# Norm roots of three head norms: spread to all rows by one rounded pass instead of a full-precision one, and the stick-breaking steps placed one tile later

## The chip, the cores and the metric

One core of one Trainium2 chip. The metric is the device time of one launch in microseconds (us), lower is better.

## The reference, cut to what matters

One decoder layer on 256 tokens of width 2048, all float32. `h = RMSNorm(x)`, one wide projection `h @ w_in` (32 column tiles of 128 for the mixers, then 48 for the gates), three mixers, a gated merge, `w_out`, and a gated MLP. What the change touches is the RMS norm over each head's 128 features, in two places: on the HGRN2 output, and on the stick-breaking mixer's queries and keys (QK-norm).

```python
# HGRN2 output, heads of 128
o = o * lax.rsqrt(jnp.mean(o * o, axis=-1, keepdims=True) + EPS)
# stick-breaking attention
qh = rms_norm(heads(q), q_g)
kh = rms_norm(heads(k), k_g)
z = jnp.einsum('bhqd,bhnkd->bhqnk', qb, kb) * scale
log_keep = jnp.where(mask, jax.nn.log_sigmoid(-z), 0.0)
within = lax.cumsum(log_keep, axis=4, reverse=True) - log_keep
w = jnp.where(mask, jnp.exp(jax.nn.log_sigmoid(z) + within + later[..., None]), 0.0)
```

## The kernel before, in words

**Layout and stream.** Features lie on the 128 partitions, tokens along the free axis. All weights stream from HBM in pieces of 128x1024 float32 through a ring of four buffers. For each piece ScalarE (ACT) writes a rounded copy `w_hi` in fp32r (line 711), VectorE (DVE) writes the rest `w_lo = raw - w_hi` (line 1024), and TensorE (PE) multiplies both parts. A wide-projection tile is two pieces; from tile 8 on it is 48 matmuls of 256 columns (line 368). In this text `lo(p)` is the w_lo operation of piece p; tile n reads pieces 2n and 2n+1.

**The order of the work.** Everything of the three mixers is put by hand between the 80 tiles of the wide projection. The table `AT` (line 92) gives each mixer product the tile after which PE issues it: `mixers(n)` of PE runs right after the matmuls of tile n. On ACT and DVE a loop over n does first the two pieces 2n+4 and 2n+5 (so they work two tiles ahead), then the eviction of tile n, then their own `mixers(n+1)`. So a result that DVE makes in `mixers(n+1)` can stand in front of lo(2n+6), which PE needs at the start of tile n+3. Every engine runs its queue in order; nothing overtakes.

**Small operations.** In DVE and ACT code each operation that a later one on the same engine depends on is issued with `link`: a semaphore increment and a wait for it before the next instruction.

**The level products.** `lev0` to `lev8` of HGRN2 stand after tiles 12, 14, 16 ... 28. For level k DVE multiplies two factors (lines 1227 and 1228), which PE waits for (line 413 is the helper that issues all full-precision products). Between tiles 7 and 16 DVE also computes the token norm, scales the first groups and x (lines 1040, 1217), splits the scaled x into `a_in` (line 1257), and does the S5 constants (`s_t`, lines 1048, 1051, 1055).

**The head norms.** `ss` (after tile 31) sums the squares of HGRN2's output, q and k: each head's sums stand on all 32 rows of its row group 32h..32h+31, with 3x256 columns (`NORM_V`). ACT takes ln and exp(-0.5 ln) in its steps 33 and 34, and DVE makes one Newton step in step 35 (`inverse_root`, three operations of 128x768, line 1048 and twice line 1055), giving `NORM_Y`. `qk_rb` after tile 35 and `hg_rb` after tile 39 (line 489) spread one row of each group over all 128 partitions with a matmul of 32 rows: weights `first_rows` (1 in the first row of each 32, else 0, set by five POOL memsets), moving data `NORM_Y` in float32. `qk_rb` has 8 such products (q and k, four heads) and `hg_rb` 4; a float32 matmul appears as two records in the trace. The four heads use four different row groups and four different PSUM banks. DVE then scales q and k (line 1273) or HGRN2's output (line 1286).

**The stick-breaking steps.** `z0`, `z1` after tile 37; ACT copies them out in step 38 (line 813) and takes abs, exp and ln(1+.) of 128x1536 with two table loads; DVE in step 39 makes softplus and log-sigmoid (line 1055, 128x1536, twice) and masks four slices (line 1048, in place on tmp); in step 40 come, in the order of the code, the scaling of HGRN2's output (line 1286, twice) and `softp_lo` (twice); `hg_out` (line 1055, four times) in step 41. `within0`, `within1` stand after tile 41, the subtraction (line 1314) in step 42, the exp in ACT's step 42, the mask `sb_w` in DVE's step 43, and `sb_o` after tile 44. The S5 states use DVE in steps 44 to 49 (rotation, scans, rotation back) behind `bu0`, `bu1`, which stand after tile 43; `o_split` is in DVE's step 48. Products alternate between two PSUM pairs in the order of `AT`, and a product waits until the one two places before it was read.

**Buffers.** `T[i]` are seven 128x1024 scratch slots of `tmp`. `NORM_Y` is in T[6]. T[4] holds the masks' index data in the first steps, HGRN2's factors later, and the softplus from DVE's step 39 on.

Of the kernel before, what the change touches and what calls it, by code (L numbers as in the profile page):

```python
# [38 lines left out]
F32 = mybir.dt.float32  # L39
F32R = mybir.dt.float32r  # L40
I32 = mybir.dt.int32
U8 = mybir.dt.uint8
ALU = mybir.AluOpType
ACT = mybir.ActivationFunctionType

P = 128
HALF = P // 2
D_MODEL = 2048
SEQ = 256
BW = D_MODEL // 4  # L50
HEADS = BW // P
# [37 lines left out]
assert all(x % RING == 0 for x in (GLU_P, BR_P, OUT_P, UP_P, DOWN_P, GLU_T, BR_T, OUT_T, UP_T, DOWN_T))  # L89


AT = {"norm1": 7, "s5_bT": 20, "hg_vT": 15, "hg_o": 30, "ss": 31, "sb_vT": 34, "qk_rb0": 35, "qk_rb1": 35, "hg_rb0": 39, "hg_rb1": 39,
      "z0": 37, "z1": 37, "within0": 41, "within1": 41, "sb_o": 44}
AT.update({f"lev{k}": 12 + 2 * k for k in range(LEVELS + 1)})
STATES_AT = (43, 46, 51, 54, 59, 62, 67, 70)
AT.update({f"bu{k}": STATES_AT[k - k % 2] for k in range(8)})
# [36 lines left out]
def layer(nc, xT, w_in, w_glu, w_br, w_out, w_up, w_down, norm_mix, norm_ffn, hg_gain, s5_small, s5_b, s5_c,  # L133
          s5_skip, sb_gain, conv, out):
    ctx = ExitStack()
    with ctx:
        def sb(name, shape, dt=F32, scope=None):
            return (scope or ctx).enter_context(nc.sbuf_tensor(name, shape, dt))
# [4 lines left out]
        w_lo = [sb(f"w_lo{s}", [P, PIECE * P], F32R) for s in range(RING)]  # L143
        half = [sb(f"half{s}", [P, SEQ]) for s in range(2)]
        ones = sb("ones", [P, P], F32R)
        first_rows = sb("first_rows", [P, P])
        eye = sb("eye", [P, P])
        upper = sb("upper", [P, P])
        lower = sb("lower", [P, P], F32R)
# [34 lines left out]
        s5_bT = sb("s5_bT", [P, 2, CT, P], F32, early)  # L184
# [7 lines left out]
        within = ExitStack()  # L192
        sb("below_within", [P, 3 * CT * SEQ + 2 * 1024], F32, within)
        softp_hi = sb("softp_hi", [P, 2 * 1024], F32R, within)
        softp_lo = sb("softp_lo", [P, 2 * 1024], F32R, within)
        within.close()
        splits = ExitStack()
        gated = sb("gated", [P, 6, SEQ], F32, splits)
# [18 lines left out]
        s5_b_in, s5_bb = proj1[:, 1, :, :], flat(proj1[:, 2, :, :])  # L217
        T = [tmp[:, i, :] for i in range(7)]
        T4 = [t.rearrange("p (c t) -> p c t", c=4) for t in T]
        NORM_V, NORM_Y, NORM_T1 = T[2][:, 0:3 * SEQ], T[6][:, 0:3 * SEQ], T[0][:, 0:3 * SEQ]  # L220
        T2 = [tmp[:, i, :].rearrange("p (s t) -> p s t", t=P) for i in range(7)]


# [9 lines left out]
        def S(name):  # L233
            if name not in sems:
                sems[name] = ctx.enter_context(nc.semaphore(name))
            return sems[name]
# [10 lines left out]
        def link(eng, ins, name):  # L247

            counts[name] = counts.get(name, 0) + 1
            ins.then_inc(S(name), 1)  # L250
            eng.wait_ge(S(name), counts[name])
# [94 lines left out]
        def _(pe):  # L346
# [99 lines left out]
            def mixers(n):  # L446
# [32 lines left out]
                for name, parts in (("qk_rb", (1, 2)), ("hg_rb", (0,))):  # L479
                    if n == AT[name + "0"]:  # L480

                        pe.wait_ge(S("norms_rstd"), 1)
                        pe.wait_ge(S("first_rows"), 1 + HEADS)
                        outs_ = [start_product(f"{name}{e}") for e in range(2)]
                        for c, part in enumerate(parts):
                            for h in range(HEADS):
                                rows = slice(32 * h, 32 * h + 32)
                                at = 512 * (h % 2) + c * SEQ
                                mm = pe.matmul(outs_[h // 2][:, at:at + SEQ], first_rows[rows, :], NORM_Y[rows, part * SEQ:(part + 1) * SEQ],
                                               start=True, stop=True, skip_group_check=True)  # L490
                                if part == parts[-1] and h % 2:
                                    mm.then_inc(product_done, 1)
# [23 lines left out]
                if n == AT["sb_o"]:  # L516
# [5 lines left out]
                    for h in range(HEADS):  # L522
                        at = 768 * (h // 2)
# [4 lines left out]
                for c in range(CT):  # L528
                    if n == AT[f"bu{2 * c}"]:
# [4 lines left out]
                        outs_ = [start_product(f"bu{2 * c + e}") for e in range(2)]  # L534
                        for r in range(2):
                            for i in range(4):
                                rows = slice(32 * i, 32 * i + 32)
# [145 lines left out]
        def bc(x, shape):  # L683
            return x.broadcast_to(shape)
# [12 lines left out]
        def s5v(name):  # L697
            return s5_t[:, SIDX[name], :]
# [5 lines left out]
        def _(act_e):  # L704
# [15 lines left out]
            def run(name, out_, in_, func, **kw):  # L720
                link(act_e, act_e.activation(out_, in_, func, **kw), name)  # L721
# [19 lines left out]
            def mixers(n):  # L741
# [62 lines left out]
                    run("norms_root", NORM_Y, NORM_V, ACT.Ln)  # L804
                if n == AT["ss"] + 3:
                    run("norms_root", NORM_Y, NORM_Y, ACT.Exp, scale=-0.5)
                if n == AT["sb_vT"] + 1:
                    wait_product(act_e, "sb_vT")
                    taken(act_e.activation(flat(HG_QQ), product("sb_vT")[:, :], ACT.Copy), "sb_vT")
# [208 lines left out]
        def _(ve):  # L1018
# [38 lines left out]
            def inverse_root(name, v, y, t):  # L1057

                ve.wait_ge(S(name + "_root"), 2)
                tt(name + "_newton", t, y, y, ALU.mult)  # L1060
                stt(name + "_newton", t, t, -0.5, v, ALU.mult, ALU.mult)
                stt(name + "_rstd", y, t, 1.5, y, ALU.add, ALU.mult)
# [29 lines left out]
            def exp_scale(out_):  # L1092

                c, n_, p = "s5_setup", s5v("t1"), s5v("t3")
                bits = s5v("r").bitcast(I32)
                ts(c, n_, n_, -126.0, 127.0, ALU.max, ALU.min)
                ts(c, bits, n_, 127.0, None, ALU.add)
                ts(c, bits, bits, 23, None, ALU.logical_shift_left)
                stt(c, out_, p, 1.0, s5v("r"), ALU.add, ALU.mult)
# [74 lines left out]
            def mixers(n):  # L1174
# [22 lines left out]
                if n == 7:  # L1197
                    masks(2)
                    exp_scale(s5v("mag"))
                if n == 12:  # L1200
                    ve.wait_ge(S("late_landed"), 16 * 9)
                    s5_angle()
# [61 lines left out]
                    ts("sb_gain", gain_sb[:, 0:1], gain_sb[:, 0:1], P ** -0.5, None, ALU.mult)  # L1264
                if n == AT["ss"] + 4:
                    inverse_root("norms", NORM_V, NORM_Y, NORM_T1)
                if n == AT["qk_rb0"] + 1:
                    for e in range(2):
                        wait_product(ve, f"qk_rb{e}")
                        heads = slice(2 * e, 2 * e + 2)  # L1270
                        rb = product(f"qk_rb{e}").rearrange("p (h c t) -> p c h t", h=2, c=2)
                        for c, x in enumerate((SQ, SK)):
                            ins = ve.scalar_tensor_tensor(x[:, heads, :], x[:, heads, :], gain_sb[:, c:c + 1], rb[:, c], ALU.mult, ALU.mult)
                            if c == 0:
                                issue(ins, "q_normed")
                            else:
                                taken(ins, f"qk_rb{e}")
                    settle(ve, "q_normed")
                    for e in range(2):
                        wait_taken(ve, f"qk_rb{e}")  # L1280
# [299 lines left out]
        def _(pool):  # L1580
            def tt(name, out_, a, b, op):
                link(pool, pool.tensor_tensor(out_, a, b, op), name)
# [1 line left out]

            link(pool, pool.memset(ones[:, :].bitcast(F32), 1.0), "ones")
            link(pool, pool.memset(s5_cT[:, :, :, :, :], 0.0), "s5_zero")
            link(pool, pool.memset(first_rows[:, :], 0.0), "first_rows")
            for h in range(HEADS):
                link(pool, pool.memset(first_rows[32 * h:32 * h + 1, :], 1.0), "first_rows")
            link(pool, pool.memset(T[3], 0.0), "hg_ex0")  # L1590
            ints = T[4].bitcast(I32)
            for c, (step, mult) in enumerate(((1, -1), (1, 0), (0, 1), (0, 1))):
# [136 lines left out]
```

## Time and profile before

| what | value |
|---|---|
| median of 3 runs | 1402.86 us (1402.77 to 1404.02) |
| the profiled execution | 1402.92 us, its span on the core 1401.4 us |
| granted TensorE clock | 1.000 of full speed over the span |
| busy shares PE, DVE, ACT, POOL | 99%, 74%, 54%, 10% |
| matmul records | 9682 |
| DMA mean | 187 GB/s |

The profile gives, for one execution, each instruction's start and duration, what each engine waited for, and the chain of work that ended last. Starts of matmuls are recorded, their ends are modelled: two matmuls in a row overlap in the table, so the distance between starts is what a matmul costs.

### The profile page before, as it was taken

The page shows a single profiled execution, that of the slowest core. Times are in us where ns is not written, and L with a number is a line of the kernel's source. Part 1 is how long each engine was busy: PE and PEld are TensorE (multiplying, and loading weights), DVE is VectorE, ACT ScalarE, POOL GpSimd, SP SyncE. Part 2 cuts the span into 40 slices and gives each one's busy share as a digit, 9 for nine tenths or more (in the row PEclk, how much of TensorE's full clock was granted, in tenths as well). Part 3 has the DMA queues.
Part 4 walks back from the last instruction along what each step waited for, and adds up shares of the span by engine and source line. Part 5 has one row for each costly group of instructions (what it writes and reads, how often), then busy time and mean ns, then how long its engine had stood idle before and what let it go on. Part 6 is the DMA issues. An engine that isn't in the chain of part 4 may idle for free.

```text
span 1401.4 us, 27481 instructions
## 1 busy us (share of the span) xinstructions
PE 1394.3 (99%) x9682; PEld 1285.5 (92%) x9682; DVE 1030.6 (74%) x1409; ACT 754.0 (54%) x1050; POOL 143.4 (10%) x190
## 2 busy tenths in 40 slices
PE   9999999999999999999999999999999999999999
PEld 8999999999999999988888888888888888888888
DVE  7898866699898777776687777777777776445453
ACT  7584777654543454545555555555555554344332
POOL 1200000000000014322111111111111110000000
PEclk9999999999999999999999999999999999999999
DMA  8654545454555556665556656656656656666663
GB/s 280 191 181 168 162 153 184 147 168 165 189 178 174 195 171 223 223 192 194 170 197 196 189 186 192 192 180 193 191 187 193 190 177 194 208 185 202 194 206 109
DMA packets 75935, 261.66 MB, mean 187 GB/s; under 512 B 8736, under 2 KB 9280, under 8 KB 75872
## 3 DMA queue, kind: packets, MB, share of 16 engines
q1 hardware_dynamic: 74304, 256.41, 57.0%
q0 software_dynamic: 1424, 4.37, 1.1%
q8 instruction: 44, 0.72, 0.2%
q14 instruction: 19, 0.16, 0.0%
q10 hardware_dynamic: 144, 0.01, 0.0%
HBM read 258.66 MB, written 2.10 MB: 186 GB/s over the span
## 4 chain that ended last, share of the span: by engine, by line
PE 91%; DVE 6%; ACT 2%; DMA 1%; issue 0%; SPq 0%; ACTq 0%; DVEq 0%
PE bank L354 40%; PE bank L368 22%; PE bank L356 21%; PE bank L394 5%; DVE w_lo L1024 2%; PE pair L413 1%; PE bank L379 1%; DVE a_in L1257 0%; ACT gates L721 0%; ACT w_hi L711 0%; DMA x_first<-xT 0%; DVE tmp L1055 0%; DVE tmp L1048 0%; DVE x_first L1217 0%; ACT tmp L721 0%
## 5 line engine op out<-in xcount | busy, mean ns | idle before, releaser
L1024 DVE TENSOR_TENSOR w_lo<-raw,w_hi 128x1024 fp32r<-128x1024 f32 x496 | 584.6, 1189 | 305.3 <-ACT w_hi L711 301.5
L711 ACT ACTIVATE w_hi<-raw 128x1024 fp32r<-128x1024 f32 x496 | 508.3, 1030 | 417.0 <-PE bank L356 198.9
L354 PE MATMUL bank<-h,w_hi 128*128 128x512 f32 x1408 | 488.4, 390 | 0.0
L356 PE MATMUL bank<-h,w_lo 128*128 128x256 f32 x1408 | 397.1, 282 | 0.0
L368 PE MATMUL bank<-a_in,w_hi 128*128 128x256 f32 x2048 | 363.1, 281 | 0.5 <-DVE w_lo L1024 0.5
L368 PEld LDWEIGHTS bank<-a_in,w_hi 128*128 128x128 f32 x2048 | 311.8, 188 | 5.3 <-issue 4.6
L354 PEld LDWEIGHTS bank<-h,w_hi 128*128 128x128 f32 x1408 | 264.2, 188 | 55.4
L368 PE MATMUL bank<-a_in,w_lo 128*128 128x256 f32 x1024 | 285.5, 279 | 0.0
L356 PEld LDWEIGHTS bank<-h,w_lo 128*128 128x128 f32 x1408 | 266.1, 189 | 0.0
L354 PE MATMUL bank<-act,w_hi 128*128 128x512 f32 x660 | 228.8, 390 | 0.0
L368 PEld LDWEIGHTS bank<-a_in,w_lo 128*128 128x128 f32 x1024 | 192.5, 188 | 0.0
L356 PE MATMUL bank<-act,w_lo 128*128 128x256 f32 x660 | 186.1, 282 | 0.0
L354 PEld LDWEIGHTS bank<-act,w_hi 128*128 128x128 f32 x660 | 123.8, 188 | 26.0
L356 PEld LDWEIGHTS bank<-act,w_lo 128*128 128x128 f32 x660 | 124.7, 189 | 0.0
L1653 POOL TENSOR_TENSOR padded<-sum_u,rstd 128x256 f32<-128x256 f32 x88 | 73.7, 838 | 413.3 <-DVE sum_u L1045 400.5
L354 PE MATMUL bank<-a_in,w_hi 128*128 128x512 f32 x256 | 88.8, 390 | 0.0
L356 PE MATMUL bank<-a_in,w_lo 128*128 128x256 f32 x256 | 72.2, 282 | 0.0
L964 ACT ACTIVATE silu<-convd 128x256 f32<-128x256 f32 x43 | 17.9, 417 | 96.0 <-DVE convd L1512 96.0
L1510 DVE SCALAR_TENSOR_TENSOR convd<-padded,taps,convd 128x256 f32<-128x256 f32 x88 | 62.6, 712 | 1.0 <-ACT convd L984 1.0
L1512 DVE SCALAR_TENSOR_TENSOR convd<-padded,taps,convd 128x256 f32<-128x256 f32 x88 | 53.9, 613 | 11.5
L354 PEld LDWEIGHTS bank<-a_in,w_hi 128*128 128x128 f32 x256 | 48.0, 188 | 10.0
L718 ACT ACTIVATE half<-bank 128x256 f32<-128x256 f32 x135 | 49.2, 365 | 3.8 <-PE bank L356 3.7
(222 smaller groups left out, 1370.3 us busy)
## 6 DMA issues: line engine op xcount, KB each, us to landing
raw<-w_up SPq DMA_DIRECT2D x176, 512.0 KB, 3.8
raw<-w_in SPq DMA_DIRECT2D x156, 512.0 KB, 4.3
raw<-w_down SPq DMA_DIRECT2D x80, 512.0 KB, 4.2
raw<-w_out SPq DMA_DIRECT2D x32, 512.0 KB, 4.2
raw<-w_br SPq DMA_DIRECT2D x16, 512.0 KB, 3.5
raw<-w_br SPq DMA_DIRECT2D x16, 256.0 KB, 3.4
raw<-w_down SPq DMA_DIRECT2D x16, 256.0 KB, 2.7
x_first<-xT SPq DMA_DIRECT2D x8, 256.0 KB, 6.6
```

Source lines behind the costliest of these rows:

```text
L354: pe.matmul(bank[b][:, :], w[:, k * P:(k + 1) * P], a.rearrange("p a t -> p (a t)"), start=first and n == 0, stop=False, skip_group_check= ...
L356: mm = pe.matmul(bank[b][:, 0:SEQ], l[:, k * P:(k + 1) * P], a[:, 0, :], start=False, stop=last and n == len(blocks) - 1, skip_group_check ...
L368: mm = pe.matmul(bank[n % BANKS][:, 0:SEQ], x[:, k * P:(k + 1) * P], src[:, PIECE * h + k, part, :], start=h == 0 and k == 0 and m == 0, s ...
L379: mm = pe.matmul(bank[b][:, 0:SEQ], x[:, k * P:(k + 1) * P], rhs(k, part), start=first and k == 0 and m == 0, stop=last and k == blocks - ...
L394: mm = pe.matmul(bank[b][:, 0:SEQ], x[:, cols], src[:, k, part, :], start=k == 0 and m == 0, stop=k == CT - 1 and m == 2, skip_group_check ...
L711: act_e.activation(w_hi[s][:, 0:blocks * P], raw[s][:, 0:blocks * P], ACT.Copy).then_inc(hi_ready, 1)
L718: act_e.activation(half[j % 2][:, :], bank[j % BANKS][:, SEQ:2 * SEQ], ACT.Copy).then_inc(half_copied, 1)
L964: act_e.activation(silu[:, :], convd[:, (j - 3) % 4, :], ACT.Silu).then_inc(S("silu_done"), 1)
L1024: ve.tensor_tensor(w_lo[s][:, w], raw[s][:, w], w_hi[s][:, w].bitcast(F32), ALU.subtract).then_inc(lo_ready, 1)
L1510: ve.scalar_tensor_tensor(c, padded[:, j % 2, 1:SEQ + 1], taps[:, t, 1:2], c, ALU.mult, ALU.add).then_inc(S("tap1"), 1)
L1512: ve.scalar_tensor_tensor(c, padded[:, j % 2, 0:SEQ], taps[:, t, 0:1], c, ALU.mult, ALU.add).then_inc(S("conv_done"), 1)
L1653: pool.tensor_tensor(padded[:, j, 2:], sum_u[:, j, :], rstd[:, :], ALU.mult).then_inc(S("up_scaled"), 1)
```

## The change

It does four things. (1) The weights become `two_rows`, in fp32r: 1 in the first row of each group of 32, -1 in the second, 0 elsewhere. DVE makes them in its step 9, from the row index that POOL left in T[4], with seven linked operations: six on 128x1 and one on 128x128. The five POOL memsets of `first_rows` go. (2) The root is kept as a rounded part and a remainder: ACT copies `NORM_Y` rounded into `NORM_HI` (128x768) in step 36, and DVE writes `norm_rows = NORM_Y * second_row + NORM_HI` (128x768) in its step 36, which holds hi in the first row and -(lo) in the second. One fp32r matmul of 32 rows then gives hi + lo. (3) `qk_rb` and `hg_rb` read `norm_rows`, so each of the 12 products is one fp32r pass. (4) `qk_rb` goes from tile 35 to 36, `z0`/`z1` from 37 to 38, `within0`/`within1` from 41 to 42 and `sb_o` from 44 to 45, with all ACT and DVE steps that are given relative to them. `hg_rb` stays at 39. `NORM_Y` moves to T[4], `norm_rows` is in T[6], `NORM_HI` in T[5].

```diff
-AT = {"norm1": 7, "s5_bT": 20, "hg_vT": 15, "hg_o": 30, "ss": 31, "sb_vT": 34, "qk_rb0": 35, "qk_rb1": 35, "hg_rb0": 39, "hg_rb1": 39,
-      "z0": 37, "z1": 37, "within0": 41, "within1": 41, "sb_o": 44}
+AT = {"norm1": 7, "s5_bT": 20, "hg_vT": 15, "hg_o": 30, "ss": 31, "sb_vT": 34, "qk_rb0": 36, "qk_rb1": 36, "hg_rb0": 39, "hg_rb1": 39,
+      "z0": 38, "z1": 38, "within0": 42, "within1": 42, "sb_o": 45}
...
-        first_rows = sb("first_rows", [P, P])
+        two_rows = sb("two_rows", [P, P], F32R)
+        second_row = sb("second_row", [P, 1])
...
+        norm_rows = sb("norm_rows", [P, 1024], F32R, within)
...
-        NORM_V, NORM_Y, NORM_T1 = T[2][:, 0:3 * SEQ], T[6][:, 0:3 * SEQ], T[0][:, 0:3 * SEQ]
+        NORM_V, NORM_Y, NORM_T1 = T[2][:, 0:3 * SEQ], T[4][:, 0:3 * SEQ], T[0][:, 0:3 * SEQ]
+        NORM_HI, NORM_ROWS = softp_lo[:, 1024:1024 + 3 * SEQ], norm_rows[:, 0:3 * SEQ]
...
-                        pe.wait_ge(S("norms_rstd"), 1)
-                        pe.wait_ge(S("first_rows"), 1 + HEADS)
+                        pe.wait_ge(S("norm_rows"), 1)
+                        pe.wait_ge(S("two_rows"), 7)
...
-                                mm = pe.matmul(outs_[h // 2][:, at:at + SEQ], first_rows[rows, :], NORM_Y[rows, part * SEQ:(part + 1) * SEQ],
+                                mm = pe.matmul(outs_[h // 2][:, at:at + SEQ], two_rows[rows, :], NORM_ROWS[rows, part * SEQ:(part + 1) * SEQ],
                                                start=True, stop=True, skip_group_check=True)
...
+                if n == AT["ss"] + 5:
+                    act_e.wait_ge(S("norms_rstd"), 1)
+                    run("norm_hi", NORM_HI, NORM_Y, ACT.Copy)
...
+                if n == 9:
+                    row, part, first = (T[4][:, (c + 1) * P - 1:(c + 1) * P] for c in (2, 3, 4))
+                    row, part = row.bitcast(I32), part.bitcast(I32)
+                    for size in (HALF, P // 4):
+                        ts("two_rows", part, row, float(size), float(size), ALU.is_ge, ALU.mult)
+                        tt("two_rows", row, row, part, ALU.subtract)
+                    ts("two_rows", second_row[:, :], row, 1.0, -1.0, ALU.is_equal, ALU.mult)
+                    ts("two_rows", first, row, 0.0, None, ALU.is_equal)
+                    tt("two_rows", two_rows[:, :], bc(first, [P, P]), bc(second_row[:, 0:1], [P, P]), ALU.add)
...
+                if n == AT["ss"] + 5:
+                    ve.wait_ge(S("norm_hi"), 1)
+                    stt("norm_rows", NORM_ROWS, NORM_Y, second_row[:, 0:1], NORM_HI.bitcast(F32), ALU.mult, ALU.add)
...
-            link(pool, pool.memset(first_rows[:, :], 0.0), "first_rows")
-            for h in range(HEADS):
-                link(pool, pool.memset(first_rows[32 * h:32 * h + 1, :], 1.0), "first_rows")
```

## Rows read from the trace of the kernel before

**Rows 1.** The page, part 1: busy time of each engine.
```profile
PE 1394.3 (99%) x9682; PEld 1285.5 (92%) x9682; DVE 1030.6 (74%) x1409; ACT 754.0 (54%) x1050; POOL 143.4 (10%) x190
```
**Rows 2.** Waits of PE: who was waited for, us in total, times, longest.
```profile
PE pair L413 <- DVE tmp L1228: 1.6, 3, 1.2
...
PE bank L368 <- DVE w_lo L1024: 0.5, 1, 0.5
```
**Rows 3.** Chain that ended last, 53 to 109 us: start, us, what.
```profile
53.80 5.67 PE bank L368 x48
...
65.16 1.13 DVE proj L1040
...
108.45 0.61 DVE tmp L1228
```
**Rows 4.** Timeline of DVE and PE, 93 to 110 us.
```profile
93.60 0.69 DVE L1228 TENSOR_TENSOR tmp<-tmp 128x512 f32<-128x512 f32 x1
...
94.48 1.15 PE L413 MATMUL pair<-tmp 128*64 128x64 f32 x32
...
109.11 1.15 PE L413 MATMUL pair<-tmp 128*64 128x64 f32 x32 [1.19 <-DVE tmp L1228]
```
**Rows 5.** Timeline of DVE, small linked operations.
```profile
27.51 0.17 DVE L1051 TENSOR_SCALAR s_t<-s_t 128x16 f32<-128x16 f32 x1
27.72 0.17 DVE L1055 SCALAR_TENSOR_TENSOR s_t<-s_t,s_in 128x16 f32<-128x16 f32 x1
...
46.31 0.28 DVE L1051 TENSOR_SCALAR tmp<-tmp 128x64 int32<-128x64 int32 x1
46.63 0.48 DVE L1048 TENSOR_TENSOR tmp<-tmp 128x64 int32<-128x64 int32 x2
...
215.51 0.15 DVE L1051 TENSOR_SCALAR gain_sb<-gain_sb 128x1 f32<-128x1 f32 x1
215.70 2.36 DVE L1024 TENSOR_TENSOR w_lo<-raw,w_hi 128x1024 fp32r<-128x1024 f32 x2
```
**Rows 6.** Timeline of PE around the two spreading products.
```profile
230.84 0.27 PE L368 MATMUL bank<-a_in,w_lo 128*128 128x256 f32 x1
231.04 1.15 PE L489 MATMUL pair<-tmp,first_rows 32*128 32x256 f32 x16
232.12 0.50 PE L368 MATMUL bank<-a_in,w_hi 128*128 128x256 f32 x2
...
257.44 0.71 PE L489 MATMUL pair<-tmp,first_rows 32*128 32x256 f32 x8
258.09 0.51 PE L368 MATMUL bank<-a_in,w_hi 128*128 128x256 f32 x2
```
**Rows 7.** Timeline of DVE and ACT, 228 to 236 us.
```profile
228.72 1.95 DVE L1055 SCALAR_TENSOR_TENSOR tmp<-tmp 128x768 f32<-128x768 f32 x2
...
232.17 0.36 ACT L739 ACTIVATE gates<-bank 128x256 f32<-128x256 f32 x1
...
235.31 1.06 ACT L711 ACTIVATE w_hi<-raw 128x1024 fp32r<-128x1024 f32 x1 [2.77 <-PE bank L368]
```
**Rows 8.** Chain that ended last, 243 to 273 us: start, us, what.
```profile
243.69 2.63 PE pair L413 x16
...
255.47 2.36 DVE w_lo L1024 x2
...
264.53 5.85 PE bank L368 x48
270.37 2.29 PE pair L413 x16
```
**Rows 9.** Timeline of DVE behind the masks, 265 to 273 us.
```profile
265.44 1.27 DVE L1286 TENSOR_TENSOR proj<-proj,pair 128x512 f32<-128x512 f32 x2
266.80 1.95 DVE L1048 TENSOR_TENSOR softp_lo<-tmp,softp_hi 128x768 fp32r<-128x768 f32 x2
...
271.06 2.04 DVE L1055 SCALAR_TENSOR_TENSOR proj<-proj,gain_hg 128x256 f32<-128x256 f32 x4
```

## The prediction, made before the changed kernel ran

> **What bounds the kernel now.** The page's first part says it at once: PE is busy 99% of the span, DVE 74% and ACT 54% [rows 1]. So I read next what PE waits for. All its waits on DVE together are a few us, of which two kinds bear on this change: 1.6 us in three waits for the level factors of line 1228, the longest 1.2, and one wait of 0.5 us for a `w_lo` [rows 2]. The average share hides what these two are, so I read the chain that ended last. For most of the span it is PE's own matmuls, one wide tile being 48 matmuls in 5.67 us, 0.118 us each [rows 3]. In two stretches it leaves PE. From 59.95 us the chain runs down DVE alone, operation behind operation; in the view it is DVE from 65.16 to the end of line 1228 at 109.06, and PE's level product starts at 109.11 after waiting 1.19 us [rows 3, 4]. The level product before it stands in the same way right behind DVE: line 1228's operation begins at 93.60 and, if it takes 0.61 us as its like in the chain does, ends by 94.3, PE begins at 94.48 [rows 3, 4]. The second stretch begins with the end of `z1` at 246.32, goes over ACT's chain and DVE's softplus and masks, and comes back to PE at 264.53, where tile 41 starts 0.5 us late [rows 2, 8]. So the question for each edit is whether it lies on PE, on one of these two DVE stretches, or beside them.
>
> **Setting up two_rows: 1.55 us, on the path.** Seven linked operations enter DVE's step 9, which is the stretch that begins before line 1040 at 65.16 [rows 3]. Six are on one column. The nearest row is one column too: it starts at 215.51 and the next operation at 215.70, so 0.19 us a step. With 16 columns a step is 0.21 (27.51 to 27.72) [rows 5]. The two `is_ge, mult` on integers are dearer: at 64 columns the step is 0.32 (46.31 to 46.63), against 0.24 to 0.26 for the integer subtraction beside it, so I add 0.05 for each [rows 5]. That is 6 x 0.19 + 2 x 0.05 = 1.24. The seventh has 128 columns and two inputs: on the line between the 0.24 of 64 columns [rows 5] and the 0.61 of 512 [rows 3] lies 0.3, which I take. Sum 1.55; bounds 1.4 and 1.7. DVE has no idle time from there to 109 that could take it, so `lev2`'s factors come 1.55 later, and `lev1`'s too. PE then waits 1.55 us more at `lev1`, and is late by just that when it comes to `lev2`; the two delays are one and the same and are not added. On the way the `w_lo` of tile 11 gets late by a few tenths as well, inside the same 1.55. The five memsets that POOL loses free nothing: POOL is at 10% [rows 1], and what DVE reads of its index data in its first steps is there long before.
> The Trainium skill (VectorE: DVE Perf Modes, the section on the TRN2 errata) gives a float32 tensor_tensor (N+151)/0.96 ns. As an estimate by that page this sum would be 6 x 0.16 + 0.29 = 1.25 us. The rows of one column stand above it, so I stay with them.
>
> **The spreading products: 0.58 us less for qk_rb, 0.3 for hg_rb.** With 16 records of `qk_rb` between them, two wide matmuls start 1.28 us apart (230.84 to 232.12); less the usual 0.12 it costs 1.16. For 8 records of `hg_rb` the next wide matmul starts 0.65 behind the first [rows 6]. The difference, 232.12-231.04 against 258.09-257.44, is 0.43 for 8 records, so 0.054 a record, and about 0.2 remain for entering and leaving, whatever the number. A float32 record of 256 columns with all rows costs about 0.22 (`z`, 8 of 256 and 8 of 128 columns in 2.63 us [rows 8]), so 0.054 is four row groups at work side by side. An fp32r one with all rows costs 0.118, four side by side 0.03. I take that: `qk_rb` 16 x 0.054 - 8 x 0.03 = 0.62, rounded down to 0.58 for its first loads, `hg_rb` half, 0.3. The bounds: no fp32r product of 32 rows is in the trace; if their groups do not overlap, `qk_rb` costs 8 x 0.118 = 0.94 instead of 0.86 and the gain is a loss of 0.1; if each can't start faster than 0.054 behind the other, the gain is 0.43 and 0.22.
> The Trainium skill (TensorEngine Tiling (Array Packing), Key Properties) says that a change of tiling mode drains the engine. By it the 0.2 us stay at both places with half or a quarter of the work between; the trace agrees, as its part that does not depend on the count shows.
>
> **The root's split: nothing.** ACT's copy of 128x768 comes behind the eviction at 232.17, and ACT then idles 2.77 us up to 235.31 for PE: under 1 us fits in. DVE's `norm_rows` is one 128x768 of 0.98 us [rows 7], and waits for the copy. It ends at about 234.5 in the time of before, and PE, without `qk_rb` behind tile 35, ends tile 36 at about 231.1 + 5.7 = 236.8: 2.3 us to spare. Behind the waiting DVE instruction stands lo(76), whose `w_hi` is not made before 235. If that cover were gone, the copy and the combination would cost up to 1.8. The scaling of q and k then follows a tile later, with a whole tile more before `z0`.
>
> **The tile later: 1.45 us on the path from z to the next w_lo.** `z0`/`z1` stand behind tile 38 instead of 37, and all of ACT's chain moves with them unchanged. What does not move is `hg_rb`, at 39. Before, DVE did softplus and masks in step 39, then lo(82), lo(83), then in step 40 the scaling of line 1286. Now softplus and masks are in step 40 too, and the code of line 1286 stands in front of them. DVE arrives there at 257.83 (255.47 + 2.36) in the time of before [rows 8]; ACT's logarithm stands ahead of the `w_hi` that this `w_lo` waited for, so it is done and nothing covers line 1286. It costs 266.80 - 265.44 = 1.36 [rows 9], and about 0.1 of waiting for `hg_rb`, which PE starts at 257.44 [rows 6] and now needs 0.4 us for. The path from `z1` to the `w_lo` behind the masks, now lo(84), thus grows by 1.45. Between them PE has as before three tiles and `hg_rb`, but 0.3 less of it. So PE's wait, now before tile 42, is 0.5 + 1.45 + 0.3 = 2.25 us in place of 0.5, and the 0.3 us of `hg_rb` are given back in it.
> What is late next: after lo(84), DVE does lo(85), `hg_out` and `softp_lo`, 1.1 + 2.1 + 2.0 us [rows 9], and is ready 5.1 us after tile 42 starts, 0.7 before PE wants `within` at 5.8. Then lo(86), lo(87) end at 7.4, `within` takes 2.29 [rows 8], tile 43 starts at 8.1: covered. The subtraction ends at about 11.6, `bu0` wants it at 13.8. The mask of `sb_w` (1.8) now stands in front of `bu0`'s rotation, and by my count the following `w_lo` have 2 us or more to spare each. `o_split` goes a step later into a lighter one. All DMA loads wait for a `w_lo` four pieces before theirs and move with them; nothing else is on SP's queue, and POOL issues none here.
>
> **Sum.** 1.55 + 1.45 - 0.58 = +2.4 us. The profiled execution was 1402.92 with a span of 1401.4, 0.06 above the median of 1402.86; so 1405.3 on either footing. A measurement of this kernel can tell about 0.2%, 2.8 us, from no change, so this is a small loss just inside "same".
>
> **Rivals.**
> A. *The row groups do not overlap in fp32r.* For it: no such product in the trace. Against: the float32 ones overlap, and so it is hardly a matter of type. `qk_rb` then gives +0.1 in place of -0.58, and with half a tenth more for the entry the sum is +3.1: 1406.0, slower by 0.22%. It decides from about 0.085 us a pass on. Chance 0.08.
> B. *softp_lo comes too late for within.* Place: DVE between lo(84) and `softp_lo`, where only 0.7 us are to spare. If ACT's w_hi(85) or the rounding of the softplus comes 1.7 us later than counted, PE waits 1 us more: +3.4, 1406.3, slower. Against: both are issued before they are needed in the trace of before. Chance 0.15.
> C. *The stretch of step 9 has slack after all* and takes the set-up: -1.55, so +0.85, 1403.7. Against: the chain is DVE without a break, and two PE waits stand right behind it. Chance 0.1.
> D. *Line 1286 hides*, since DVE gets to it while ACT's chain still runs: then -1.45, so +0.95, 1403.8. It would need ACT to be late by over 1 us. Chance 0.1.
> E. *Both hide*: -0.9 us, 1402.0. Still no faster by 0.2%. Chance 0.03.
> The forecast itself has 0.54. Its terms' own bounds are 0.15 for the set-up, 0.15 for `qk_rb`, 0.2 for line 1286, and the runs of before spread by 1.2 us; a fifth of it lies above 2.8. Slower by over 0.2%: 0.08 + 0.15 + a fifth of 0.54, in all 0.33 or so. Faster by over 0.2% needs 2.8 us that no row offers: 0.02. The rest, 0.65, is the same. The range takes in C and D below and B above, with a few tenths for the measurement: 1403.4 to 1406.8.
>
> **What would show it.** The profile after should show: seven small DVE operations of 1.5 to 1.6 us in all between 65 and 67 us, and `lev2` at about 110.7 with its wait as before or `lev1` with a longer one; 12 records of line 489's product instead of 24, the 8 of `qk_rb` in 0.5 us; line 1286 directly before the two 128x1536 operations; and one PE wait for `w_lo` of about 2.2 us where 0.5 was. PE's waits on DVE in all then rise from 2.1 (1.6 and 0.5) to about 5.4. I am wrong if the level products do not move, if the wait before tile 42 is under 1 us, or if a new wait stands before `within`.

## The result, and the profile after

| kernel | median us | ratio to the kernel before, 95% interval |
|---|---|---|
| before | 1402.86 (5 runs beside the changed one) | |
| changed | 1413.60 (1412.89 to 1414.72, 5 runs) | 1.0075 (1.0064 to 1.0087) |

The change costs 10.7 us (0.75%, clear of the noise) where 2.4 were forecast, and lies outside the range (1403.4 to 1406.8). The profiled execution has a span of 1411.5 us against 1401.4. The page of the changed kernel begins so (part 1, busy time; compare [rows 1]):

```profile
PE 1402.2 (99%) x9670; PEld 1283.3 (91%) x9670; DVE 1033.1 (73%) x1417; ACT 754.7 (53%) x1051; POOL 142.3 (10%) x185
```

PE has 12 records less, as announced, and is busy 7.9 us *longer*. That is the first sign of the miss: waits would not show as busy time. PE's waits are next (who was waited for, us in total, times, longest; compare [rows 2]):

```profile
PE bank L371 <- DVE w_lo L1030: 2.5, 2, 2.1
PE pair L416 <- DVE tmp L1243: 2.2, 3, 1.2
...
PE bank L357 <- DVE w_lo L1421: 0.6, 2, 0.4
```

On DVE they rise from 2.1 (1.6 and 0.5, the two kinds of the forecast) to 4.7 us, where 5.4 were forecast. The mechanisms of the forecast are there, and can be checked one by one. The seven set-up operations on DVE (timeline of the changed kernel; columns start, duration, engine, line, operation, tiles):

```profile
64.24 0.14 DVE L1057 TENSOR_SCALAR tmp<-tmp 128x1 int32<-128x1 int32 x1
64.42 0.16 DVE L1054 TENSOR_TENSOR tmp<-tmp 128x1 int32<-128x1 int32 x1
...
65.37 0.29 DVE L1054 TENSOR_TENSOR two_rows<-tmp,second_row 128x128 fp32r<-128x128 f32 x1
65.70 1.22 DVE L1046 TENSOR_TENSOR proj<-proj,rstd 128x1024 f32<-128x1024 f32 x1
```

From 64.24 to 65.70 they take 1.46 us; the forecast said 1.55. PE feels the delay in two places before `lev2` (timeline of PE in the changed kernel):

```profile
52.56 0.59 PE L416 MATMUL pair<-proj,ones 128*128 128x256 f32 x2
...
70.48 0.47 PE L371 MATMUL bank<-a_raw,w_hi 128*128 128x256 f32 x2 [0.37 <-DVE w_lo L1030]
...
94.97 1.15 PE L416 MATMUL pair<-tmp 128*64 128x64 f32 x32 [0.37 <-DVE tmp L1243]
...
109.74 1.15 PE L416 MATMUL pair<-tmp 128*64 128x64 f32 x32 [1.24 <-DVE tmp L1243]
```

The forecast had a few tenths at the `w_lo` of tile 11 (here 70.48) and 1.55 more at `lev1` (94.97); it is 0.37 at each. Counted from the start of `norm1`'s product (52.56 here, 53.20 before), `lev1` comes 1.1 us later than before and `lev2` 1.3. The spreading products on PE (timeline; compare [rows 6]):

```profile
237.69 0.28 PE L371 MATMUL bank<-a_in,w_lo 128*128 128x256 f32 x1
237.89 0.51 PE L492 MATMUL pair<-norm_rows,two_rows 32*128 32x256 f32 x8
238.33 0.50 PE L371 MATMUL bank<-a_in,w_hi 128*128 128x256 f32 x2
...
258.11 0.39 PE L492 MATMUL pair<-norm_rows,two_rows 32*128 32x256 f32 x4
258.43 0.51 PE L371 MATMUL bank<-a_in,w_hi 128*128 128x256 f32 x2
```

Between two wide matmuls `qk_rb` now takes 0.64 us in place of 1.28, `hg_rb` 0.32 in place of 0.65 from its first record on: 0.64 and 0.33 saved. The single records of the first four products, one for each row group, start at 0, 3, 6 and 10 ns: they overlap. Line 1286 of before, now 1304, in front of softplus, and PE's wait (timeline of DVE, then of PE; compare [rows 8, 9]):

```profile
263.95 1.28 DVE L1304 TENSOR_TENSOR proj<-proj,pair 128x512 f32<-128x512 f32 x2
265.33 3.55 DVE L1061 SCALAR_TENSOR_TENSOR tmp<-tmp 128x1536 f32<-128x1536 f32 x2
...
270.75 2.36 DVE L1030 TENSOR_TENSOR w_lo<-raw,w_hi 128x1024 fp32r<-128x1024 f32 x2
273.03 2.04 DVE L1061 SCALAR_TENSOR_TENSOR proj<-proj,gain_hg 128x256 f32<-128x256 f32 x4
275.10 1.95 DVE L1054 TENSOR_TENSOR softp_lo<-tmp,softp_hi 128x768 fp32r<-128x768 f32 x2
```
```profile
272.12 0.48 PE L371 MATMUL bank<-a_in,w_hi 128*128 128x256 f32 x2 [2.11 <-DVE w_lo L1030]
277.85 0.40 PE L416 MATMUL pair<-softp_hi,lower 128*128 128x512 f32 x1
```

The step costs 1.38 us (265.33 - 263.95) and the wait is 2.11 where 2.25 was forecast. `softp_lo` ends at 277.05, 0.8 us before `within`; 0.7 was forecast.

The S5 product behind all mixer steps that the change moves, `s5_y0`, starts at 329.14 us against 327.12 (the first row is of the kernel before, the second of the changed one):

```profile
327.12 1.07 PE L413 MATMUL pair<-proj,s_cT 128*32 128x256 f32 x16
```
```profile
329.14 1.07 PE L416 MATMUL pair<-proj,s_cT 128*32 128x256 f32 x16
```

That is 2.0 us, and 2.7 from the start of `norm1`'s product on; the head before it ended 0.6 us earlier in this execution (52.5 to 53.7 in the profiled executions of all kernels). The other 8.2 us come later, where no instruction differs. The windows show how (columns: the stretch, its length, then busy us and records of PE, PEld, DVE, ACT, POOL, the granted clock, DMA share, GB/s). The kernel before, in the in-projection, `w_out` and up stages:

```profile
400.00:450.00 50.00, 50.00 (x438) 48.79 (x438) 41.42 (x52) 20.07 (x26) 0.00 (x0) 1.00 0.53 178
600.00:640.00 40.00, 40.00 (x233) 35.48 (x232) 28.88 (x37) 20.57 (x30) 9.49 (x14) 1.00 0.59 184
800.00:900.00 100.00, 100.00 (x579) 88.67 (x578) 77.92 (x109) 56.40 (x91) 15.12 (x18) 1.00 0.60 189
```

The changed kernel:

```profile
400.00:450.00 50.00, 50.00 (x438) 48.79 (x437) 41.52 (x53) 19.67 (x26) 0.00 (x0) 1.00 0.58 182
600.00:640.00 40.00, 40.00 (x228) 34.85 (x227) 28.53 (x37) 19.74 (x28) 9.47 (x14) 1.00 0.60 184
800.00:900.00 100.00, 100.00 (x575) 87.60 (x574) 77.32 (x109) 56.26 (x90) 15.13 (x18) 1.00 0.61 188
```

At the same granted clock and without a wait PE starts 575 matmuls in 100 us instead of 579, and 228 instead of 233 in 40 us of the `w_out` stage. In these stages every matmul has become dearer by a little; in the in-projection, whose matmuls have 256 columns, the count stays at 438. As a finer gauge I use the distance between the starts of two successive 512-column matmuls (one 256-column matmul lies between them), averaged over 800 to 860 us of the timeline: 346.6 ns before, 348.9 ns after; over 585 to 645 us, the `w_out` stage, 346.7 and 353.4. For the in-projection I take the distance between two successive 256-column matmuls, averaged over 400 to 470 us: 117.7 and 117.8.

What differs there is only where the buffers lie. The new `second_row` needs 4 bytes per partition but gets a slot of 32, and it stands behind `two_rows`: every buffer behind it begins 32 bytes higher in each partition. The weight ring (`w_hi`, `w_lo`) lies in front and does not move; all moving operands (`a_raw`, `a_in`, `h2`, `act`, the splits) do. This gave **theory L**: the place of the buffers costs some 8 us. The rival, **theory R**: the loss comes from what the change computes or from when it does so.

### The profile page after: what moved, and what is told of

It is laid out like the page before. It is cut to its first block, busy times and chain, and to the rows that moved or that the text cites. A ratio compares the mean times of both kernels' runs of the same rounds, so it can differ in the third digit from the quotient of the medians.

```text
span 1411.5 us, 27462 instructions
## 1 busy us (share of the span) xinstructions
PE 1402.2 (99%) x9670; PEld 1283.3 (91%) x9670; DVE 1033.1 (73%) x1417; ACT 754.7 (53%) x1051; POOL 142.3 (10%) x185
## 4 chain that ended last, share of the span: by engine, by line
PE 81%; DVE 1%; issue 0%
PE bank L357 39%; PE bank L359 20%; PE bank L371 15%; PE bank L397 5%; PE bank L382 1%; PE pair L416 1%; PE pair L542 0%; DVE tmp L1061 0%; DVE tmp L1054 0%; DVE w_lo L1030 0%; DVE proj L1304 0%; DVE x L1584 0%
```

## Experiments on the place of the buffers

**Four bytes alone.** The kernel before with one line more:

```diff
         first_rows = sb("first_rows", [P, P])
+        sb("pad", [P, 1])
```


> The kernel before with nothing added but an unused buffer of 4 bytes per partition behind first_rows, as second_row is in the changed kernel. It moves every buffer behind it by 32 bytes, all of TensorE's moving operands (a_in, a_raw, h2, act, the o splits) among them; the weight ring lies in front and stays. Theory L (the place of the buffers costs the part of the loss that the change's own steps don't explain, +8 us): about 1411, and the distance from one 512-column matmul to the next in the up stage goes from 346.7 ns to 348.9. Theory R (the loss comes from what the change computes, or from where its new operations stand): 1402.9, distance 346.7 ns.

Measured: 1411.56 us against 1403.21, ratio 1.0061 (1.0047 to 1.0074). An unused buffer of four bytes costs 8.35 us. The windows of this kernel:

```profile
600.00:640.00 40.00, 40.00 (x228) 34.84 (x227) 28.11 (x35) 20.16 (x30) 9.82 (x16) 1.00 0.62 185
800.00:900.00 100.00, 100.00 (x575) 87.57 (x574) 77.51 (x108) 55.78 (x89) 15.12 (x18) 1.00 0.61 188
```

The same 228 and 575 records as in the changed kernel. Theory R falls for these 8 us.

**The change without the move.** All instructions of the changed kernel, `second_row` in the free part of another slot:

```diff
-        second_row = sb("second_row", [P, 1])
...
-        half_pi = sb("half_pi", [P, 1])
+        half_pi = sb("half_pi", [P, 2])
+        second_row = half_pi[:, 1:2]
...
-                    link(ve, ve.memset(half_pi[:, :], TWO_PI / 4), "half_pi")
+                    link(ve, ve.memset(half_pi[:, 0:1], TWO_PI / 4), "half_pi")
```


> The changed kernel, with second_row put into the second column of half_pi, whose 32-byte slot has room: every buffer is back at its address of before; all instructions stay. Theory L: 1405.3 (the steps of the prediction, +2.4) to 1405.9, and 346.7 ns between 512-column matmuls in the up stage. Theory R: 1413.6 and 348.9 ns.

Measured: 1405.56 us against 1403.21, +2.35, ratio 1.0018 (1.0009 to 1.0027). The distance in the up stage is 346.6 ns again. So the 10.7 us divide into 8.0 to 8.4 for the place of the buffers (1413.60 - 1405.56, or 10.74 - 2.35) and 2.35 for all that the change does.

**What has to move against what.** Two kernels, each the one before with an unused 4-byte buffer, in front of `raw` (everything moves, no distance between buffers changes) or directly in front of `act` and `a_in` (masks, gains, taps and the token norm's buffers stay):

```diff
+        sb("pad", [P, 1])
         raw = [sb(f"raw{s}", [P, PIECE * P]) for s in range(RING)]
```


> The kernel before with an unused 4-byte buffer in front of the first weight buffer: everything, the weight ring too, lies 32 bytes higher, and no distance between buffers changes. If the distance between the weights (w_hi, w_lo) and the moving operand counts: 1403.2, 346.7 ns from one 512-column matmul to the next in the up stage. If the moving operand's own address counts: 1411.5 and 348.9 ns, as with 4 bytes behind first_rows.

```diff
+        sb("pad", [P, 1])
         late = ExitStack()
```


> The kernel before with an unused 4-byte buffer directly in front of act and a_in: the masks, gains, taps, rstd, var and root stay where they were, and what lies 32 bytes higher is act, h2, x1, a_in, a_raw, the splits and the mixers' scratch. If it is TensorE's moving operands that count: 1411.5. If it is what VectorE and ScalarE read of taps, rstd or the gains: 1403.2.

Measured: 1402.82 against 1402.83 (1.0001, 0.9991 to 1.0011) with everything moved, and 1411.42 (1.0063, 1.0046 to 1.0080) with only the buffers from `act` on moved. Windows of the first, then of the second:

```profile
800.00:900.00 100.00, 100.00 (x579) 88.64 (x578) 77.93 (x109) 56.41 (x91) 15.11 (x18) 1.00 0.61 189
```
```profile
800.00:900.00 100.00, 100.00 (x575) 87.61 (x574) 77.31 (x109) 56.20 (x90) 15.14 (x18) 1.00 0.60 188
```

It is not the address of the moving operand that counts but its distance from the weights, or from something else that lies in front of it with them (the ring's `raw` and `half` buffers moved together with the weights in the first kernel, and stayed in the second; these runs do not part them). Nor do they part the moving operands from the other buffers that moved with them, on which DVE, ACT and POOL work.

The distance alone does not fix the pace either. In the head, from 20 to 50 us, PE multiplies `a_raw` with the ring, at the same places in the changed kernel and in the two kernels slowed by four bytes; the distance between 512-column matmuls there is 348.9 ns in the changed kernel and 353.3 in the other two. Of instructions only the five memsets of POOL are gone from the changed kernel there, and in the others they have ended by 3.5 us.

**Other distances.** The kernel before with unused buffers of 64 (shown below), 96 and 128 bytes behind `first_rows`, and with small buffers put together so that all behind them lies 32 or 64 bytes lower:

```diff
+        sb("pad", [P, 16])
```
```diff
-        skip_s5 = sb("skip_s5", [P, CT])
-        half_pi = sb("half_pi", [P, 1])
+        small = sb("small", [P, CT + 1])
+        skip_s5, half_pi = small[:, 0:CT], small[:, CT:CT + 1]
```
```diff
+        small = [sb(f"small{s}", [P, 8]) for s in range(2)]
+        gain_hg, skip_s5 = small[0][:, 0:HEADS], small[0][:, HEADS:HEADS + CT]
+        gain_sb, half_pi = small[1][:, 0:2], small[1][:, 2:3]
```


> The kernel before with an unused buffer of 64 bytes per partition behind first_rows; the moving operands then begin 32 bytes past a multiple of 64, as in the kernel before. If the place within 64 bytes is what counts in theory L: 1402.9. If it is a distance between buffers or a place within 128 or 512 bytes: another time, up to 1411. Theory R: 1402.9.

> The kernel before with an unused buffer of 96 bytes per partition behind first_rows; the moving operands then begin at a multiple of 128 bytes. If the place within 64 bytes counts in theory L: about 1411, as with 32 bytes. Otherwise another time. Theory R: 1402.9.

> The kernel before with an unused buffer of 128 bytes per partition behind first_rows. If the distance between weights and moving operand counts modulo 128 bytes: as before, 1402.9. If modulo more than that: another time. The pairs 128 bytes apart so far, +17.6 and +19.9 (plus 64, minus 64), +16.1 and +12.1 (plus 96, minus 32), are near each other but not equal, which speaks for a part that repeats and a part that does not.

> The kernel before with half_pi moved into the slot of skip_s5: everything behind lies 32 bytes lower (moving operands at a multiple of 128 bytes). No theory predicts which way; plus 32 gave +8.3 us, plus 64 +17.6, plus 96 +16.1. If the cost grows with the distance from the present place on both sides: about +8. If it grows with the address only: 1403 or less, 346.7 ns or less in the up stage. If places 128 bytes apart are alike: +16, as plus 96.

> The kernel before with gain_hg and skip_s5 in one slot and gain_sb and half_pi in another: everything behind lies 64 bytes lower. Alike 128 bytes apart: +17.6 as plus 64. Growing with the address only: 1403 or less. Growing on both sides: above the result of 32 bytes lower.

| moved by | time minus that of the kernel before | in-projection | `w_out` stage | up stage |
|---|---|---|---|---|
| -64 bytes | +19.9 us (1.0141, 1.0124 to 1.0158) | 118.3 ns | 353.3 ns | 353.4 ns |
| -32 | +12.1 (1.0087, 1.0070 to 1.0104) | 120.0 | 353.3 | 346.7 |
| 0 | | 117.7 | 346.7 | 346.6 |
| +32 | +8.35 (1.0061, 1.0047 to 1.0074) | 117.8 | 353.3 | 348.9 |
| +64 | +17.6 (1.0125, 1.0110 to 1.0141) | 120.0 | 350.0 | 350.0 |
| +96 | +16.1 (1.0116, 1.0100 to 1.0131) | 118.7 | 351.1 | 351.1 |
| +128 | +2.7 (1.0019, 1.0010 to 1.0029) | 118.6 | 346.7 | 346.7 |

The columns of ns are the distances between matmuls, as above: between 256-column ones in the in-projection, between 512-column ones in the other two stages. All six other places are slower. None of my guesses on the form holds: it is neither the place within 64 bytes (+64 keeps it and costs 17.6 us), nor the address only, nor the distance from the present place. 128 bytes away is nearly as good as zero, and what it costs lies outside the two stages with 512 columns, which run at the old pace: the in-projection takes 118.6 ns a matmul instead of 117.7, some 3 us on the 72 x 48 matmuls from tile 8 on (an estimate from these figures). The pairs 128 apart (+17.6 and +19.9, +16.1 and +12.1) are near each other but not equal. The window of the in-projection at +128, where the kernel before has 438 records:

```profile
400.00:450.00 50.00, 50.00 (x435) 48.80 (x435) 41.26 (x52) 19.55 (x25) 0.00 (x0) 1.00 0.59 183
```

The time per matmul takes a few values only, and one kernel can have different ones in the `w_out` and up stages although the matmuls are of one shape. I have no mechanism for this; the runs show the effect and its size, and no more.

## Experiments on the 2.35 us of the change itself

All three start from the changed kernel with the old places.

**The set-up where DVE waits anyway.**

```diff
                     mean("norm1", var[:, :], SEQ)
                     ve.nop().then_inc(S("norm1_var"), 1)
+                    row, part, first = (T[4][:, (c + 1) * P - 1:(c + 1) * P] for c in (2, 3, 4))
...
+                    tt("two_rows", two_rows[:, :], bc(first, [P, P]), bc(second_row[:, 0:1], [P, P]), ALU.add)
                     token_norm("norm1")
...
-                if n == 9:
-                    row, part, first = (T[4][:, (c + 1) * P - 1:(c + 1) * P] for c in (2, 3, 4))
...
```


> The changed kernel with the buffers at their places of before, and the seven operations of two_rows moved to the place where VectorE waits 2.27 us for ScalarE's root of the first norm (step 8, in front of token_norm). If the set-up costs its 1.5 us because VectorE has no slack from there to lev2: 1.5 us less than the changed kernel with the old places (+2.35 over before), so +0.9 over before. If it was hidden already: +2.35. The wait for lev2 stays about 1.2 us either way; the start of lev2 against the end of norm1 shows it.

**hg_rb a tile later too.**

```diff
-"hg_rb0": 39, "hg_rb1": 39
+"hg_rb0": 40, "hg_rb1": 40
```


> The changed kernel with the buffers at their places of before, and hg_rb after tile 40 instead of 39, so that its scaling on VectorE comes a step after softplus and masks, as before the change. If that scaling in front of softplus makes TensorE's wait before tile 42: that wait falls from about 2.1 us to 0.5 or 0.6, and the time to +0.9 over before. Rival, that hg_out and softp_lo, now both behind it, make within late: a new wait at within, and +2.

**Both.**

> The changed kernel with the old places, the set-up in VectorE's wait and hg_rb after tile 40. If the three costs are separate and these are all of them, what is left is the shorter spreading products, -0.6 and -0.3: 0.6 to 0.9 us below before, 1402.1. If something is missing in the account: at or above before.

| kernel (old places) | median us | against before, 1403.05 in the last three | PE's wait before tile 42 |
|---|---|---|---|
| the change | 1405.56 | +2.35 | 2.17 us |
| set-up in the wait | 1404.82 | +1.8 (1.0011, 1.0002 to 1.0020) | 2.17 |
| hg_rb after 40 | 1403.53 | +0.5 (1.0004, 0.9995 to 1.0013) | 0.84 |
| both | 1402.03 | -1.0 (0.9993, 0.9984 to 1.0002) | 0.84 |

Two expectations were missed. With the set-up in the wait +0.9 was expected and +1.8 measured. With `hg_rb` after 40 a wait of 0.5 to 0.6 us and +0.9 were expected, 0.84 and +0.5 measured. The wait of 0.84 is the 0.52 of before and the 0.33 that `hg_rb` is now shorter: PE arrives that much earlier at tile 42, so this saving is given back in the wait. The prediction had that term, the expectation had left it out.

**The set-up.** Its price is read from the start of `norm1`'s product to `lev2`. Without it (the kernel before; `lev2` stands at 109.11 [rows 4]), with it (`hg_rb` after 40), and with it in the wait (both):

```profile
53.20 0.59 PE L413 MATMUL pair<-proj,ones 128*128 128x256 f32 x2
```
```profile
52.62 0.59 PE L416 MATMUL pair<-proj,ones 128*128 128x256 f32 x2
...
109.94 1.15 PE L416 MATMUL pair<-tmp 128*64 128x64 f32 x32 [1.29 <-DVE tmp L1243]
```
```profile
52.49 0.59 PE L416 MATMUL pair<-proj,ones 128*128 128x256 f32 x2
...
108.42 1.15 PE L416 MATMUL pair<-tmp 128*64 128x64 f32 x32 [1.22 <-DVE tmp L1242]
```

That is 55.91, 57.32 and 55.93 us: the set-up costs 1.4 us there, and nothing in the wait. (In the profiled execution of the change with the old places the stretch is longer, 57.93: PE waits 1.12 us for the `w_lo` of tile 11 there, against 0.52 with `hg_rb` after 40, where no edit differs up to that point. With the set-up in the wait it is 56.06.) In the medians, with `hg_rb` after 40, moving the set-up too is worth 1.5 us (1403.53 to 1402.03), as expected.

**The clock.** Without `hg_rb` after 40 moving the set-up seemed worth 0.7 only. The reason stands in the windows of the profiled execution with the set-up moved, behind the 2.17 us for which PE waits before 270.51:

```profile
268.00:270.00 2.00, 0.34 (x3) 0.14 (x2) 1.90 (x4) 1.65 (x2) 0.00 (x0) 1.00 0.00 0
270.00:272.00 2.00, 1.49 (x8) 1.52 (x9) 1.96 (x4) 1.97 (x4) 0.00 (x0) 0.71 0.18 25
272.00:274.00 2.00, 2.00 (x12) 2.00 (x11) 1.89 (x4) 0.34 (x2) 0.00 (x0) 0.50 0.88 320
274.00:276.00 2.00, 2.00 (x17) 2.00 (x17) 1.93 (x3) 0.79 (x1) 0.00 (x0) 0.93 0.44 180
```

The granted clock falls to 0.50, the lower of the two levels (1.2 GHz), and is back during the fourth window. The rows of PE show the wait and then the slower pace:

```profile
270.51 0.48 PE L371 MATMUL bank<-a_in,w_hi 128*128 128x256 f32 x2 [2.17 <-DVE w_lo L1030]
...
271.65 0.63 PE L371 MATMUL bank<-a_in,w_hi 128*128 128x256 f32 x2
```

Tile 42 then takes 7.24 us up to `within` (270.51 to 277.75) in place of 5.68 in the change with the old places (272.57 to 278.25): 1.56 us. This happens in some executions and not in others: in the profiled ones of the change with the old places and of the changed kernel the clock stays at 1.00 behind waits of 2.17 and 2.11 us. What decides it is not shown. With the set-up in the wait the mean clock is below 1.000 in 9 of 11 executions, which take 1404.6 to 1405.3 us, and 1.000 in the other two, which take 1403.2 and 1403.4. With the change at the old places it is below in 4 of 11 (1406.0 to 1406.7 against 1404.3 to 1405.9), in the changed kernel in one of five (1414.72). With `hg_rb` after 40, where PE waits 0.84 us, it is never below, nor in 33 executions of the kernel before. Only the one lowered execution that was profiled shows where the clock falls; for the others there is the mean clock and the time. The times fit: the lowered executions are on average 1.6 us longer than the others with the set-up in the wait (1404.89 and 1403.29), and 1.3 longer in the change with the old places (1406.45 and 1405.14). Like compared with like, moving the set-up is worth 1.6 us between the lowered executions and 1.9 between the others (of which one side has only two). So the 1.5 us seemed halved because the clock fell in 9 of 11 executions on one side and in 4 of 11 on the other.

With both repairs the costs of the set-up, of the later tile and of the clock are gone and the shorter products remain: 1.0 us less than before, where 0.6 to 0.9 were expected. Since 0.3 are given back in the wait of 0.84 us, 0.6 is the figure that follows from the account; in the profiled executions `s5_y0` comes 0.8 us earlier, counted from `norm1`. The interval of the times takes in 1, so faster than before is likely, not shown.

## Why the prediction was wrong

- **What bounds the kernel** held: PE, with two stretches in which DVE sets its pace.
- **Setting up two_rows**, 1.55 us on the path: 1.46 by its records, 1.5 by the experiment that hides it. Right, and so was the argument that the chain has no slack there. Only where PE feels it was a little off: part of it at the `w_lo` of tile 11, less at `lev1`. The Trainium skill's figure (VectorE: DVE Perf Modes, the section on the TRN2 errata) gave 1.25, 0.2 too low. As an estimate it has 0.16 for a one-column operation; here the operations themselves take 0.14 to 0.16, but their steps, with the wait in between, are 0.18 to 0.20.
- **The spreading products**, 0.58 and 0.3: 0.64 and 0.33. The row groups overlap in fp32r too, so rival A is out. Eight records take 0.12 us more than four (0.44 and 0.32 from their first record to the next wide matmul), 0.03 each as forecast, so about 0.2 us remain that do not depend on the number. That is in accord with the drain at a change of tiling mode (the Trainium skill, TensorEngine Tiling (Array Packing), Key Properties).
- **The tile later**, 1.45 us on the path from `z` and a wait of 2.25: 1.38 for line 1304 and 2.11 to 2.17. Right. Putting `hg_rb` a tile later as well takes 1.9 us off, more than the 1.45. Against the executions whose mean clock is 1.000 alone it is 1.5 (means 1405.14 and 1403.61); the rest goes with the four executions whose mean clock is lower. That part, up to 1.6 us in an execution, was not in the sum. Rivals B to E are out: `within` has no wait, and both costs are real.
- **The sum**, +2.4: the same instructions at the old places measure +2.35. That it fits so closely is partly luck: in the executions whose mean clock is 1.000 it is +2.0 (means 1405.14 and 1403.11), and the lost clock of the other four, which no term of the sum stood for, brings the rest.
- **The step that failed** is a term that the sum 1.55 + 1.45 - 0.58 put at nothing without a word: what the change does to the price of the matmuls that it does not touch. The prediction read from the rows that most of the span is PE's own matmuls and carried that price over as it was; it has a sentence on the five memsets that go, and none on the buffer that comes. `second_row` moves the moving operands by 32 bytes against the weight ring, and the matmuls of the `w_out`, up and down stages become dearer by 0.6% to 2% (346.6 to 348.9 ns and 346.7 to 353.4): 8.35 us by itself. The diff showed the line, and the prediction never asked where it stands. Why the place changes the pace stays open.
- **The range** was built from the bounds of the steps alone and could not hold this.

## What to carry to other kernels

When a change adds, drops or resizes a buffer that stands before the operands of the bounding engine, compare the addresses before anything else, and time the kernel before with the same empty buffer: here four unused bytes cost over three times as much as all that the change does. A small persistent buffer is better put into the free part of a slot, which kept every address here; behind the large buffers it would move nothing either, but no run tried it. A wait of TensorE like the one of 2.17 us here can cost more than its length, since the clock may fall behind it. And when a step moves by a tile, look at what then comes to stand in front of it on the same engine, and move that too.

## What the runs showed of the hardware that was not expected

- The pace of fp32r matmuls depends on how far the moving operands, and what moves with them, lie from the weight ring and its neighbours. Seven places, 32 bytes apart, gave 346.6 to 353.4 ns for a 512-column and a 256-column matmul together in the up stage, 117.7 to 120.0 ns for a 256-column one in the in-projection, and up to 19.9 us on 1403. Moving all together changes nothing (1.0001).
- After a wait of 2.17 us the granted clock fell to half for some 3 us in part of the executions, which cost 1.56 us in the profiled one; with a wait of 0.84 us the mean clock was 1.000 in all 22 executions.
- Row groups in fp32r overlap as in float32: eight products of 32 rows and 256 columns take 0.52 us between wide matmuls with entry and exit, and the twelve products together save PE 0.97 us with twelve records less.
